# Mixture of experts in a four-layer network on one core: the first expert's tokens gathered by products of their own, and its up and down products placed ahead of the gate's first half and of the gathering for all experts

## The reference, cut to what matters

```python
def expert_choice_moe(x, router_w, w1, w3, w2):
    cap = EC_CAPACITY_FACTOR * s // N_EXPERTS
    aff = jax.nn.softmax(jnp.einsum('bsd,de->bse', x, router_w).astype(jnp.float32), axis=-1)
    gates, idx = lax.top_k(aff.transpose(0, 2, 1), cap)
    xg = jax.vmap(lambda xb, ib: xb[ib])(x, idx)
    hid = jax.nn.silu(jnp.einsum('becd,edf->becf', xg, w1)) * jnp.einsum('becd,edf->becf', xg, w3)
    ye = jnp.einsum('becf,efd->becd', hid, w2) * gates[..., None].astype(x.dtype)
    return jax.vmap(lambda yb, ib: jnp.zeros((s, d), x.dtype).at[ib.reshape(-1)].add(yb.reshape(-1, d)))(ye, idx)
```

## Time and profile before

| what | value |
|---|---|
| median of 3 runs | 2350.19 us (2348.97 to 2354.24) |
| the profiled execution's own time | 2356.38 us |
| its span in the trace | 2354.6 us |
| TensorE products busy | 2036.1 us, 86% of the span |
| VectorE / ScalarE / GpSimd busy | 1022.7 / 722.6 / 92.8 us |
| DMA | 623.84 MB, 265 GB/s over the span |
| chain that ended last | PE 55%, DMA 31%, DVE 7%, ACT 4%, POOL 1% |

### The profile page before, as it was taken

The page is one execution under the profiler, slowest core; times in us unless marked ns, Lnnn a source line. Parts: engine busy times, 40 slices in busy tenths (PEclk is TensorE's granted clock), DMA queues, the critical chain, the costliest instruction groups (busy, mean ns, idle before and its releaser), DMA issues.

```text
span 2354.6 us, 31441 instructions
## 1 busy us (share of the span) xinstructions
PE 2036.1 (86%) x12764; PEld 1387.1 (59%) x12764; DVE 1022.7 (43%) x1487; ACT 722.6 (31%) x1090; POOL 92.8 (4%) x150
## 2 busy tenths in 40 slices
PE   9999777777788987777778999989999999989998
PEld 6765222222265642222224887977887888877886
DVE  4652000000276420000004776766776776666666
ACT  5533100000145320000002333454333433454332
POOL 0000000000020000000000000020000000020000
PEclk9999989988999998899899999989999999999999
DMA  5459999999952699999998555325563664434650
GB/s 190 152 221 422 426 426 426 426 426 427 412 195 86 256 423 426 426 427 426 426 427 293 196 179 191 116 88 186 172 210 129 197 204 170 127 107 147 210 174 32
DMA packets 195840, 623.84 MB, mean 265 GB/s; under 512 B 17622, under 2 KB 129336, under 8 KB 163000
## 3 DMA queue, kind: packets, MB, share of 16 engines
q1 hardware_dynamic: 195768, 622.84, 68.4%
HBM read 621.76 MB, written 1.05 MB: 265 GB/s over the span
## 4 chain that ended last, share of the span: by engine, by line
PE 55%; DMA 31%; DVE 7%; ACT 4%; POOL 1%; issue 1%; SPq 1%; DVEq 0%; POOLq 0%; ACTq 0%
DMA weight_ring<-in_w 29%; PE psum L2708 14%; PE psum L613 11%; PE psum L2682 10%; PE psum L2711 7%; PE psum L2162 4%; PE psum L2179 2%; PE psum L2207 2%; DMA weight_ring<-in_ple_gate_w 1%; SPq L174 1%; PE psum L2189 1%; PE psum L2347 1%; DVE x_both L492 1%; ACT w_hi L574 1%; ACT arena L2543 0%
## 5 line engine op out<-in xcount | busy, mean ns | idle before, releaser
L2162 PE MATMUL psum<-weight_ring,arena 128*32 128x256 f32 x4096 | 286.4, 436 | 129.9 <-DMA weight_ring<-in_w 129.9
L2708 PE MATMUL psum<-x_both,up_hi 128*128 128x512 f32 x1408 | 355.3, 394 | 3.1 <-DVE x_both L492 2.9
L2162 PEld LDWEIGHTS psum<-weight_ring,arena 128*32 128x32 f32 x4096 | 135.8, 122 | 282.3 <-DMA weight_ring<-in_w 169.5
L2708 PEld LDWEIGHTS psum<-x_both,up_hi 128*128 128x128 f32 x1408 | 257.3, 188 | 58.7 <-DVE x_both L492 4.5
L2179 PE MATMUL psum<-weight_ring,arena 128*32 128x512 f32 x1024 | 238.0, 641 | 50.4 <-DMA weight_ring<-in_w 43.1
L2262 DVE TENSOR_TENSOR arena<-arena,psum 128x256 f32<-128x256 f32 x32 | 13.5, 421 | 509.2 <-PE psum L2162 509.2
L613 PE MATMUL psum<-w_hi,x_both 128*128 128x384 f32 (+3 forms) x896 | 216.9, 374 | 9.3 <-DVE mix_lo L746 6.2
L2756 DVE TENSOR_TENSOR up_lo<-weight_ring,up_hi 128x2048 fp32r<-128x2048 f32 x88 | 201.3, 2292 | 18.7 <-ACT up_hi L2730 18.1
L2711 PEld LDWEIGHTS psum<-x_both,up_lo 128*128 128x128 f32 x1408 | 190.1, 188 | 13.8
L2711 PE MATMUL psum<-x_both,up_lo 128*128 128x256 f32 x1408 | 193.9, 280 | 0.0
L2768 DVE TENSOR_REDUCE arena<-psum 128x256 f32<-128x512 f32 x176 | 113.4, 686 | 180.2 <-PE psum L2711 179.6
(11 more groups left out here) (353 smaller groups left out, 2294.4 us busy)
## 6 DMA issues: line engine op xcount, KB each, us to landing
weight_ring<-in_w SPq DMA_DIRECT2D x192, 2048.0 KB, 25.7
weight_ring<-in_ffn_wg SPq DMA_DIRECT2D x44, 1024.0 KB, 5.5
weight_ring<-in_ffn_wu SPq DMA_DIRECT2D x44, 1024.0 KB, 8.0
weight_ring<-in_ffn_wd SPq DMA_DIRECT2D x44, 1024.0 KB, 5.0
weight_ring<-in_w_in SPq DMA_DIRECT2D x14, 1536.0 KB, 6.9
weight_ring<-in_w_o SPq DMA_DIRECT2D x4, 2048.0 KB, 16.5
weight_ring<-in_ple_gate_w SPq DMA_DIRECT2D x4, 2048.0 KB, 11.2
weight_ring<-in_w_out SPq DMA_DIRECT2D x4, 2048.0 KB, 7.9
```

Source lines behind the costliest of these rows:

```text
L2162: last = pe.matmul(ps[j * CAP:(j + 1) * CAP, 4 + k // 2, 0:QW], tokens_now[:, cc, :], w[:, c, j * QW:(j + 1) * QW], start=cc == 0, stop=cc ...
L2708: last = pe.matmul(ps[:, 4 + 2 * f + h, :], w_part[:, f, h, c, :], x_both[:, :, c, :], start=c == 0, stop=False, skip_group_check=True)
```

## The change

For the first expert alone, `gather_first` makes its tokens by 32 products like those of the gathering but with 32 streamed columns in place of 512, into bank 4; ScalarE copies them straight to `tokens_now`. Its up and down products follow. Then come the gate's first half, the gathering for all experts (`gather_all`), expert 1's up products, all eight groups of `turn_back`, the clearing of the banks, the scatter of expert 0, expert 1's down products, its scatter, and the gate's second half. The first gate half's split weights lie elsewhere in the arena (`early_quarters`), and `rows_lo` lies in `ln_params`; so the layer norm's gain and bias (`ln2_g`, `ln2_b`, 512 KB each) are loaded after `gather_all`, on the SP queue behind T8, no longer before the experts.

```diff
-    rows_hi, rows_lo = over("rows_hi", "x_cols", 0, TILES, D), over("rows_lo", "arena", LOOP_AT, TILES, D)
+    early_quarters = tuple(tuple(over(f"early_{part}_{i}", "arena", (2 * i + j) * D, D)[:, :] for j, part in
+                                 enumerate(("hi", "lo"))) for i in range(2))
+    rows_hi, rows_lo = over("rows_hi", "x_cols", 0, TILES, D), over("rows_lo", "ln_params", 0, TILES, D)
...
-            tile_ready(sp, 1)
-            load_params(sp, (ln_params[:, 0, :], spread(t["ln2_g"][layer])),
-                        (ln_params[:, 1, :], spread(t["ln2_b"][layer])))
...
+        def gather_first(pe):
+            for c in range(DC):
+                for a in range(TILES):
+                    for part in (rows_hi, rows_lo):
+                        last = pe.matmul(ps[:, FIRST_BANK, c * CAP:(c + 1) * CAP], part[:, a, bass.ds(c, P, DC)],
+                                         one_hot[:, a, 0:CAP], start=a == 0 and part is rows_hi,
+                                         stop=a == TILES - 1 and part is rows_lo)
+            last.then_inc(first_gathered.sem, 1)
...
         def _(sp):
+            stream.issue(sp, early[1] + WEIGHT_SLOTS + 1)
+            sp.wait_ge(gathered.sem, gathered.at(DC))
+            for row, name in enumerate(("ln2_g", "ln2_b")):
+                sp.dma_start(ln_params[:, row, :], spread(t[name][layer])).then_inc(norm_rows.sem, 16)
             stream.issue(sp, first + WEIGHT_SLOTS)
...
+            pe.wait_ge(ple_vk.sem, ple_vk.at(4))
+            gather_first(pe)
+            first_at, second_at = at_early(0), at_early(1)
+            tokens_for(pe, first_at)
+            up(pe, early[0], arrived_early)
+            down(pe, early[0], arrived_early, first_at)
+
+            pe.wait_ge(part_0.sem, first_at(part_0, 1))
+            pe.wait_ge(part_1.sem, first_at(part_1, 1))
+            gate_products(pe, 0)
+            gather_all(pe)
+            tokens_for(pe, second_at)
+            up(pe, early[1], arrived_early)
             pe.wait_ge(four.sem, four.at(TILES))
...
+            turn_back(pe, range(EXPERTS // 2))
+            pe.wait_ge(spread_kept.sem, spread_kept.at(EXPERTS // 2))
...
+            scatter(pe, first_at)
+            pe.wait_ge(ple_added.sem, ple_added.at(1))
+            down(pe, early[1], arrived_early, second_at)
+            scatter(pe, second_at)
+            gate_products(pe, 1)
...
+            act.wait_ge(first_gathered.sem, first_gathered.at(1))
+            act.copy(tokens_now, ps[:, FIRST_BANK, 0:DC * CAP].rearrange("p (c s) -> p c s", c=DC)
+                     ).then_inc(token_set.sem, 1)
...
-            for n in range(GATE_HALVES):
-
-                set_tokens(n, early[n] if n == 0 else early[n - 1] + 4)
-                if n == 0:
-                    pool.wait_ge(spread_kept.sem, spread_kept.at(EXPERTS // 2))
-                set_back(n, early[n] + 1)
+            set_tokens(1, early[0] + 4)
+            pool.wait_ge(spread_kept.sem, spread_kept.at(EXPERTS // 2))
+            set_back(0, early[0] + 4)
+
+            pool.wait_ge(scattered.sem, scattered.at(2))
+            set_back(1, early[1] + 4)
```

More of the change, by code:

```diff
@@ L2143, in quarter_places @@
         def quarter_places(k):
-            high, low = gate_quarters[k % 2]
+            high, low = (early_quarters if k < QUARTERS else gate_quarters)[k % 2]
             return high, low, [v.rearrange("p (c n) -> p c n", c=2) for v in (high, low)]
@@ L2295, in keep_back, with gather_all @@
                          ).then_inc(spread_kept.sem, 1)
-        FIRST_TURNS, LAST_TURNS = range(4), range(4, EXPERTS // 2)
+        first_gathered, norm_rows = signal("first_tokens_gathered"), signal("norm_rows_loaded")
+        FIRST_BANK = 4
+        def gather_first(pe):
[6 more added lines that the diff above has]
+            last.then_inc(first_gathered.sem, 1)
+        def gather_all(pe):
+            for c in range(DC):
+                if c >= 4:
+                    pe.wait_ge(kept.sem, kept.at(c - 3))
+                for a in range(TILES):
+                    for part in (rows_hi, rows_lo):
+                        last = pe.matmul(ps[:, c % 4, :], part[:, a, bass.ds(c, P, DC)], one_hot[:, a, :],
+                                         start=a == 0 and part is rows_hi,
+                                         stop=a == TILES - 1 and part is rows_lo)
+                last.then_inc(gathered.sem, 1)
         @block.sync
         def _(sp):
+            stream.issue(sp, early[1] + WEIGHT_SLOTS + 1)
+            sp.wait_ge(gathered.sem, gathered.at(DC))
+            for row, name in enumerate(("ln2_g", "ln2_b")):
+                sp.dma_start(ln_params[:, row, :], spread(t[name][layer])).then_inc(norm_rows.sem, 16)
             stream.issue(sp, first + WEIGHT_SLOTS)
@@ L2341, in _ @@
             pe.wait_ge(rows_low.sem, rows_low.at(TILES))
-            for c in range(DC):
-                if c >= 4:
-                    pe.wait_ge(kept.sem, kept.at(c - 3))
-                for a in range(TILES):
-                    for part in (rows_hi, rows_lo):
-                        last = pe.matmul(ps[:, c % 4, :], part[:, a, bass.ds(c, P, DC)], one_hot[:, a, :],
-                                         start=a == 0 and part is rows_hi,
-                                         stop=a == TILES - 1 and part is rows_lo)
-                last.then_inc(gathered.sem, 1)
@@ L2352, in _ @@
-            pe.wait_ge(four.sem, four.at(TILES))
-            turn_back(pe, FIRST_TURNS)
-            pe.wait_ge(ple_vk.sem, ple_vk.at(4))
-            for n in range(GATE_HALVES):
-                at = at_early(n)
-                tokens_for(pe, at)
-                up(pe, early[n], arrived_early)
-                if n == 0:
-                    turn_back(pe, LAST_TURNS)
-                else:
-                    pe.wait_ge(ple_added.sem, ple_added.at(n))
-                down(pe, early[n], arrived_early, at)
-                if n == 0:
-                    pe.wait_ge(spread_kept.sem, spread_kept.at(EXPERTS // 2))
-                    for b in range(4):
-                        pe.matmul(ps[:, b, :], zeros_bf[:, 0:P], zeros_bf[:, :], start=True, stop=False,
-                                  skip_group_check=True)
-                scatter(pe, at)
-                gate_products(pe, n)
+            pe.wait_ge(ple_vk.sem, ple_vk.at(4))
@@ new lines, in _ @@
+            turn_back(pe, range(EXPERTS // 2))
+            pe.wait_ge(spread_kept.sem, spread_kept.at(EXPERTS // 2))
+            for b in range(4):
+                pe.matmul(ps[:, b, :], zeros_bf[:, 0:P], zeros_bf[:, :], start=True, stop=False,
+                          skip_group_check=True)
+            scatter(pe, first_at)
[3 more added lines that the diff above has]
+            gate_products(pe, 1)
@@ L2393, in _ @@
                 activate(act, at, early[n], fixed)
-                if n == 0:
-                    keep_back(act, LAST_TURNS)
+                if n == 1:
+                    keep_back(act, range(EXPERTS // 2))
                 keep_hidden(act, at)
@@ L2400, in _ @@
                 activate_gates(act, n)
+                if n == 0:
+                    for c in range(DC):
+                        act.wait_ge(gathered.sem, gathered.at(c + 1))
+                        act.copy(picked_cols[:, c], ps[:, c % 4, :].rearrange("p (e s) -> p e s", e=EXPERTS)
+                                 ).then_inc(kept.sem, 1)
             with act.Fori(0, LOOPED) as e:
@@ L2510, in _ @@
         def _(dve):
-            params_ready(dve)
+            dve.wait_ge(norm_rows.sem, norm_rows.at(0))
             for h in range(2):
```

8 lines of the change are left out of this document (1 added, 7 removed).

## The result

| | kernel before | the change |
|---|---|---|
| median of 8 runs | 2351.89 us (2345.73 to 2442.77) | 2359.14 us (2357.19 to 2363.87) |
| profiled execution, its own time / span | 2356.38 / 2354.6 us | 2357.19 / 2355.4 us |

The ratio of the change to before is **1.0037, 95% interval 1.0024 to 1.0051**: slower, by about 8.7 us (the medians differ by 7.3; the ratio leaves out the one disturbed run of before, 2442.77). The forecast was 2359.6 us, 9.4 above before; that the times agree within 0.5 us is in part luck, because the forecast started from a median of before that was 1.7 us lower (2350.19), and the differences are 9.4 against 8.7 or 7.3.

A forecast was written before the change was run, and what follows sets the result against it. In the expert stages TensorE waits for weights from saturated DMA, so the last late transfer sets each stage's end. Median 2350.2 plus 5.4 (order) plus 4.0 (clock) gave 2359.6 us, range 2346 to 2363.5.

The forecast's parts named there:

- Step 1: First expert's own gathering: 32 narrow products 7.8 us, up products 8.3 us from the start, 2.9 and 1.6 us earlier.
- the narrow gathering is short: Rival: strided loads can be hidden, the first gathering takes 3.4 us, total 2346.8 us; chance 0.13.
- T1: Weight transfer issued once expert 0's first up quarter frees a slot: forecast at 169.3 and 792.6 us.
- Step 2: TensorE's path from expert 0's up products to expert 1's: 35.6 us, before 31.0; a weight slot 1.1 us late.
- Step 3: From expert 1's up products to the last late weight slot, 40.3 us: +2.0 us in layer 0, +3.4 in layer 1.
- Step 4: Low clock through the narrow gathering into expert 0's up products: 2.0 us per layer, +4.0 us in all.
- the order at full clock: Later stage ends in both layers from TensorE's new order, without any clock loss: +5.4 us.
- A longer chain in step 3: Rival: for instance a late weight arrival pushes the second gate half, +2 us more, 2362 us; chance 0.10.

The follow-up runs named there:

- the kernel with everything together: The change plus contiguous weight loads, low rows by GpSimd, 128 columns in the first gathering, nine more idle products a layer, split turn_back: 2344.49 us, ratio 0.9992.
- the last pair of kernels: The kernel with everything together, but expert 1's up products before the gathering for all, norm's loads later: 2342.2 us (0.9973); without nine idle products 2349.4 (0.9999).

## Why the prediction was right, step by step

**Step 1, the narrow gathering: right.** 7.8 us and 8.3 to the up products were forecast; 7.81 and 7.80, and 8.26 and 8.25, came out. The products stand 0.24 us apart, with 32 streamed columns at the low clock (0.238) and with 256 at full clock: the load of strided weights sets the pace. The rival "the narrow gathering is short" would have been true of contiguous loads at full clock alone (3.80 us with the rows stored otherwise). By "TensorE: Matmul & The Clock Gate", section LDWEIGHTS, of the Trainium skill, whose cost knows no stride, it would have been 3.4 us, an estimate (32 loads of 128 columns at 1.2 GHz); the trace disagrees for this stride and agrees for contiguous rows at full clock (0.11 us).

**T1.** 169.3 and 792.6 us were forecast, that is 10.2 us behind the gathering; it was 11.58 and 11.74, because the first quarter of the up products too ran at 1.2 GHz. Step 4 had that in its price, not step 1. So T1's lead on before was 1.6 and 0.1 us and not 2.9 and 1.6.

**Step 2: right.** From expert 0's up to expert 1's up 35.6 us were summed at full clock; the change took 37.0 and 36.9, with 1.3 and 1.5 of it the clock. T8 was to be 1.1 us late: it came 35.7 and 35.4 behind T1, where 34.5 was due, so 1.2 and 0.9 late; it landed 7.2 and 6.5 us behind T7. Of the two dips of the DMA share that were forecast, this one came; ahead of T14 the landings show none.

**Step 3: TensorE's part right within half a us, the queue's part not quite.** 40.3 us from expert 1's up to T15's slot: 37.87 + 1.9 = 39.8. `turn_back` and its first transposition, 4.6 us forecast, took 4.64 (211.23 to 215.87), bound by ScalarE's eight copies in 4.02. Slot and queue were forecast level, at 243.3 and 243.1 us, and came out level. But that the norm's loads cost nothing as long as TensorE's order sets T15 was put too sharply: with them the transfers land without a gap up to T15, without them T15 lands 0.6 and 1.0 us earlier. In the kernel with everything together, where the slot is free earlier, they cost 1.2 us in layer 1 by the rule: 78.7 with them, 77.5 (the slot) without.

**Step 4, the clock: the mechanism was right, the size too large.** 2.0 us per layer were taken; the kernel with 256 columns puts it at 1.1 and 1.4. The value had been chosen between what was seen, 1.2, and 5.6; what came was near the lower end: the clock came back 2.7 and 3.1 us into the up products (169.8 and 794.5 us). What step 4 left open, whether weight loads count as activity, has an answer here: at the same spacing of loads the clock stayed low with 32 columns and returned with 256, so the loads alone did not keep it up. What the prediction takes there from the Trainium skill, "TensorE: Matmul & The Clock Gate", Part 1, agrees with that as far as it goes.

**The sum.** +9.4 us forecast; the runs say +8.7 (5.6 to 12.0 by the interval, 7.3 by the medians), the distances in the traces +6.9: +4.3 for the order at full clock (forecast 5.4, by the kernel with 256 columns, T15 +1.7 and +2.6) and +2.5 for the clock (forecast 4.0). Both terms were sized too large, the order by 1.1 us and the clock by 1.5, so no error hid another in the traces' sum. "A longer chain in step 3" did not occur: T8 had landed at 216 us and the gate's second half began at 230.91, straight behind the scatter. The remaining 1.8 us between traces and runs is inside the spread of single executions, and stays unassigned; that the kernels without the norm's loads and with the low rows on GpSimd also lose more in their runs than in their traces leaves room for a loss outside the stages that no trace here shows.

## What to carry to other kernels

A product with few streamed columns costs what its weight load costs: before narrowing one, look at how far apart the products start and whether the weights are strided. In a stage fed by a ring of slots, write down for each later slot when the queue comes to it and when it is freed; moving work off the first slot's path helps only until the next one (here T1 before, T15's slot and the queue behind T8 level in the change, T8 with everything together) is the latest. And a step made lighter can cost the clock of the step behind it: in the last pair of kernels nine idle products a layer ahead of the gathering made the difference of 0.26%, some 6 us, and without them all the reordering came out level with before.

## What the runs showed of the hardware that was not expected

- Contiguous loads of 128 weight columns follow the granted clock: 0.11 us apart at 2.4 GHz, 0.21 at 1.2 GHz. Loads at a step of eight float32 elements do not: 0.238 us at 1.2 GHz with 32 streamed columns, 0.24 at 2.4 GHz with 256.
- A copy that reads float32 at a step of eight elements took ScalarE 2.18 us instead of 1.07, VectorE 2.03 instead of 1.22 for 128x1024.
- Products of 256 and of 32 columns cost nearly the same time behind the same strided loads (8.0 and 7.8 us for 32), but only the wide ones brought the clock back; the 32-column ones let it fall 1.1 us behind their start even in layer 1, where it had been at 1.00 until then.
- 128-column products kept the clock only with more idle products ahead of them. Without these it fell as they began (at 158.6 and 783.3 us, the gatherings at 159.11 and 783.00), and their 7 us did not bring it back.
